# Attention stage of a hybrid backbone: where TensorE issues the first map of scores within a turn

## What is computed

```python
# differential attention: two maps of scores a head, 4 heads, 64 wide each
s = einsum('bqhmd,bkhmd->bhmqk', q, k) * DIFF_SCALE
p = softmax(s)
attn = p[:, :, 0] - lam * p[:, :, 1]
o = rms_norm(einsum('bhqk,bkhe->bqhe', attn, v)) * silu(gd)
# hyena, order 2, twice for each of 4 blocks of 128 channels
y = irfft(rfft(u, 2L) * rfft(filter)) + bias * u
```

## Time and profile before

| | |
|---|---|
| median of 3 runs | 3881.94 us (3874.04 to 3882.35) |
| profiled execution, its own time | 3885.88 us |
| its span, first to last instruction | 3884.1 us |
| mean granted TensorE clock | 0.949 |
| matmuls; DVE; ACT; GpSimd instructions | 18212; 4480; 1981; 782 |

### The profile page before, as it was taken

How to read it: one execution, slowest core, us unless ns; L and a number is a source line. 1 busy time by engine, 2 the same in 40 slices (tenths; PEclk the granted TensorE clock), 3 DMA queues, 4 the chain that set the end, 5 groups by cost and what they waited for, 6 DMA issues and landing times. The chain is left out here.

```text
span 3884.1 us, 48584 instructions
## 1 busy us (share of the span) xinstructions
PE 3384.3 (87%) x18212; PEld 2751.6 (71%) x18212; DVE 2470.1 (64%) x4480; ACT 1093.9 (28%) x1981; POOL 1067.4 (27%) x782
## 2 busy tenths in 40 slices
PE   6999999999868886886997899999999688858798
PEld 2787888888757775554783577888887587745477
DVE  4134577755369996885664324657775599968765
ACT  2111222212245454332210211222211455523321
POOL 4233334333212321210222423433433022232121
PEclk8999999999989998998998899999999799979899
DMA  5254223223173312344435155323322633133442
GB/s 208 65 155 147 80 91 96 86 89 97 53 204 98 84 58 71 118 113 132 146 97 206 58 122 174 99 78 103 95 90 62 199 90 93 43 107 110 128 143 69
DMA packets 414893, 423.34 MB, mean 109 GB/s; under 512 B 57040, under 2 KB 351440, under 8 KB 413506
## 3 DMA queue, kind: packets, MB, share of 16 engines
q1 hardware_dynamic: 368676, 315.22, 28.2%
q10 hardware_dynamic: 45984, 105.01, 7.7%
HBM read 287.76 MB, written 124.01 MB: 106 GB/s over the span
## 5 line engine op out<-in xcount | busy, mean ns | idle before, releaser
L754 PE MATMUL l_p_acc<-l_u_hi,l_w_hi 128*128 128x512 f32 (+1 forms) x2208 | 605.7, 376 | 22.8 <-PEq L158 9.0
L754 PE MATMUL l_p_acc<-l_u_hi,l_w_lo 128*128 128x512 f32 (+1 forms) x2208 | 587.3, 367 | 0.0
L754 PE MATMUL l_p_acc<-l_u_lo,l_w_hi 128*128 128x512 f32 (+1 forms) x2208 | 586.7, 367 | 0.0
L754 PEld LDWEIGHTS l_p_acc<-l_u_hi,l_w_hi 128*128 128x128 f32 x2208 | 383.8, 189 | 99.2 <-issue 25.2
L667 POOL TENSOR_TENSOR l_w_hi<-l_wt,l_p_zero 128x1024 fp32r<-128x1024 f32 x100 | 200.5, 2005 | 899.7 <-PE l_p_acc L754 744.1
L754 PEld LDWEIGHTS l_p_acc<-l_u_lo,l_w_hi 128*128 128x128 f32 x2208 | 380.8, 189 | 71.7
L754 PEld LDWEIGHTS l_p_acc<-l_u_hi,l_w_lo 128*128 128x128 f32 x2208 | 380.5, 189 | 71.6
L1506 PE MATMUL l_at_pS<-l_at_k_hi,l_at_q 128*128 128x512 f32 (+1 forms) x400 | 166.6, 416 | 133.1 <-ACT l_at_prob L1622 75.6
L669 POOL TENSOR_TENSOR l_w_lo<-l_wt,l_w_hi 128x1024 fp32r<-128x1024 f32 x100 | 265.3, 2653 | 7.8
L1740 DVE TENSOR_REDUCE l_at_nmax<-l_at_pS 128x1 f32<-128x1280 f32 (+1 forms) x144 | 197.4, 1371 | 103.0 <-PE l_at_pS L1507 99.0
L2457 PE MATMUL l_o_pA<-l_o_w_hi,l_o_o_hi 128*128 128x512 f32 x576 | 223.7, 407 | 42.7 <-DVE l_o_o_lo L2567 31.6
(11 more groups left out here) (331 smaller groups left out, 7058.5 us busy)
## 6 DMA issues: line engine op xcount, KB each, us to landing
l_wt<-w_in SPq DMA_DIRECT2D x104, 512.0 KB, 3.9
l_n_wa<-w_ada SPq DMA_DIRECT2D x10, 2048.0 KB, 16.5
kf_d<-l_p_R SPq DMA_DIRECT2D x72, 256.0 KB, 3.6
xbc_d<-l_p_fin ACTq DMA_DIRECT2D x28, 640.0 KB, 2.9
l_at_K<-kf_d SPq DMA_DIRECT2D x64, 256.0 KB, 2.9
l_o_rows<-w_out SPq DMA_DIRECT2D x32, 512.0 KB, 4.9
l_o_oT<-o_d SPq DMA_DIRECT2D x16, 1024.0 KB, 7.0
qk_d<-l_p_late ACTq DMA_DIRECT2D x12, 1280.0 KB, 4.6
```

What stands on the lines that cost most here:

```text
L754: mm = pe.matmul(acc[:, a:a + w], (w_hi, w_lo)[wp][m % 2][:, k], (u_hi, u_lo)[up][:, k, t0 + c:t0 + c + w], start=(k == n == 0), stop=(k = ...
```

## The change

At the end of turn `i`, between `turn_rows` and `backward(n)`, PE issues the first map of scores of unit `i + 1`; the call at the head of a turn is left for unit 0 alone. The number of instructions is the same, and so is the order on every other engine.

```diff
                 for i in range(NI):
                     n = step_of(i)
                     turning = batches[i - 2] if 2 <= i < NU + 2 else 0
+                    if i == 0:
+                        scores(i, 0)
                     if turning > 1:
                         turn(i - 2, 0, False)
-                    if i < NU:
-                        scores(i, 0)
                     if n is not None:
                         forward(n)
                     if turning > 2:
@@
                             pe.wait_ge(gated, i - 3)
                         turn_rows(r)
+                    if i + 1 < NU:
+                        scores(i + 1, 0)
                     if n is not None:
                         backward(n)
```

## The result

| | before | after |
|---|---|---|
| median, 4 runs each | 3882.14 us | 3913.99 us (3910.16 to 3920.37) |
| ratio after to before, 95% interval | | 1.0079 (1.0063 to 1.0095) |
| profiled execution, its own time | 3885.88 us | 3910.16 us |
| its span | 3884.1 us | 3908.4 us |

The account below looks back on a forecast made before the run. PE's closed ring from `exp` to `exp` was taken to bound ordinary turns, DVE's chain every fourth. Layer 1 13.4, layer 0 16.4 and clock 6.6 sum to 36.4 us over 3881.94: 3918.3 us, range 3898 to 3938.

Parts of the forecast that it names:

- The cover: Ordinary turns: only batch 0, no longer the map too, hides `copy_back` before the way there; 0.50 us a turn.
- The wait: Turn 21: the moved map's last piece waits 2.6 us for `exp(21, 1)`, ahead of the way back; 1.84 for turns 20 and 21.
- The turns with rows: There `turn_rows` already waits behind `maximum(i, 1)`, so the moved map finds its bank nearly free; two turns cost one 0.50.
- The clock: PE drops to 1.2 from 2.4 GHz behind two of three long waits; 4 x 1.65 = 6.6 us, bounds 0 and 9.9.
- heavy waits: Six waits of about 2.6 us where PE idled 1.09: turns 17, 21, 25, 29 in layer 1, 17 and 25 in layer 0.
- By layers: Covers and waits summed by groups of turns: layer 1 13.4 us, layer 0 16.4 us, together 29.8.
- Turns 34 to 38: Layer 0: the moved map delays batch 0, which starts ACT's chain to `exp`; 3.9 us, between 0 and 6.2.
- every turn falls: Rival: ordinary turns' idle of 1.57 also lowers the clock, some 30 more turns paying 1.65; 3968 us, chance 0.05.
- the 1.07 would swallow the gap: Rival: the 0.50 comes out of PE's idle at the last piece, leaving only the waits; 3889 us, chance 0.08.
- the maximum, coming sooner, would free `exp`: Rival: scores 2.15 us sooner let `exp(i, 0)` start sooner; 0.3 us in each of 60 turns, 3864 us, chance 0.05.
- PE's ring: Ordinary turn, `exp` to `exp`: 10.66 us, PE in all but 1.07 and 1.13; added PE idle lengthens the turn by as much.

Follow-up runs that it names:

- e1: Changed kernel, but the map back at its old place behind turns with n % 4 == 2 from turn 17 on; 3896.2 us, ratio 1.0028 to before.
- e3: Kernel before, with the next unit's first map moved behind the way back, still ahead of batch 0; 3886.0 us, ratio 1.0000.
- e4: Kernel before, with two of the first map's three pieces moved ahead of the way back, the last behind batch 0; 3889.0 us, ratio 1.0003.
- e2: Kernel before, with the map moved ahead of the way back only behind turns with n % 4 == 2 from turn 17 on; 3903.7 us, ratio 1.0046.
- e6: Changed kernel, with transposes and three value blocks filling PE's idle ahead of the second map's last piece; 3922.0 us, ratio 1.0099 to before.
- e5: Kernel before, with transposes and three value blocks filling PE's idle ahead of the second map's last piece; 3885.2 us, ratio 1.0007.
- e8: Kernel before; in turns with n % 4 == 2 from 9 on, two pieces of the next first map precede rows and way back; 3875.7 us, ratio 0.9977.
- e7: Kernel e5 plus the edit of e8; 3878.6 us, ratio 0.9978 to before.

## Why the prediction was right, point by point

**The cover.** Forecast 0.50 a turn, with the way there 0.86 behind batch 0. Measured 0.52 (10.66 to 11.18), 0.85, and in brackets the 0.25 of the earlier trace rows. That row, from the only turns of before in which this order already occurred, carried the largest term. `e1` shows that it costs alone, `e3` that it vanishes with the map behind the way back, `e4` that 0.59 of cover in place of 0.36 leaves 0.29 in an ordinary turn. Where DVE places the next `exp`, a smaller loss than this is absorbed (`e4`), and this one in part (`e1`: three lost covers cost 1.0 in four turns).

**The wait.** Forecast 2.6 us of idle and 1.84 for turns 20 and 21; measured 2.30 and 24.94 - 23.07 = 1.87. The idle was too large in the main because I held `exp(21, 1)` at its place against turn 20's start, 17.66; it came at 3301.61 - 3284.14 = 17.47. Already `exp(20, 1)` came 3.53 behind `exp(20, 0)` and not 3.71, released by DVE both times; that DVE had caught up in turn 20 is my reading of it. That 1.84 and 1.87 agree so closely is in part luck: from `exp(21, 1)` to the next turn's `exp` I had 7.25 and it took 7.47, as the last piece and the way there, each behind a wait, took 0.35 and 1.89 where I had 0.23 and 1.78. The two errors cancel. The turn behind took 11.26, 0.14 less than before and not 0.24, with 0.34 ahead of the way there in place of 0.25.

**The turns with rows.** Forecast: one 0.50 for two turns, an idle that shrinks to 1.6, and up to 3.3 us back. In turns 9 and 13 of layer 1 the idle was 1.59 and the turns went from 15.04 and 15.03 to 13.40 and 13.41: the whole 3.3 came back. The sum had left it out. That the shorter idle did it is likely and not shown turn by turn: with 2.10 the clock also held in turn 9 of `e2` and turn 13 of `e3`, where nothing had been changed ahead of that wait.

**The clock.** Forecast: the clock falls behind four of six heavy waits, at 1.65 each. It fell behind three. Windows behind the waits of turns 17, 21, 25, 29 of layer 1 (column PEclk is the one behind the five busy times):

```profile
3254.10:3258.10 4.00, 4.00 (x21) 4.00 (x22) 3.94 (x13) 0.06 (x1) 0.00 (x0) 0.57 0.01 4
...
3303.08:3307.08 4.00, 3.75 (x31) 3.51 (x32) 3.93 (x13) 1.63 (x6) 0.00 (x0) 1.00 0.04 12
...
3350.48:3354.48 4.00, 3.75 (x31) 3.51 (x32) 3.93 (x13) 1.65 (x6) 0.00 (x0) 1.00 0.00 0
...
3397.87:3401.87 4.00, 4.00 (x22) 3.90 (x22) 3.93 (x13) 0.26 (x1) 0.00 (x0) 0.62 0.00 0
```

The same idle of 2.30 gave 0.57 and 0.62 in two turns and 1.00 in two; of layer 0's two one fell. A turn whose clock fell took 15.37 and 15.18, else 13.76: 1.61 and 1.42. The Trainium skill (TensorE: Matmul & The Clock Gate, "HAM oscillation — how this bites in real kernels") describes a loop with a wait for a DMA of some 3 to 5 us in every round, where the clock falls in every round. The waits of 2.30 us here are shorter and did so in half of the rounds; those of 2.99 to 3.43 in `e2` did so in all six, those of 3.43 and 3.44 in `e6` in five of six.

**By layers.** Layer 1: forecast 13.4 without the clock, measured 14.3 with two falls (3.0) and the 3.3 back. Layer 0: forecast 16.4, measured 13.8 with one fall. Two errors of opposite sign lie in it. Turns 22 and 23, which I had counted at 0.5 each, became 3.8 shorter; they were long before, with idle and a low clock, and I had not asked why. Turn 13 cost 1.5, where I had 0, and turn 33, which I had left out of the six, 2.9. Turns 34 to 38 cost 2.9 where I took 3.9; of it 0.91 each are turns 34 and 38. The step that was mis-sized most, though the total stayed inside the range, is this one: the turns around short tiles were estimated, not read turn by turn.

**The rivals.** That every turn falls was wrong: ordinary turns, with 1.07 and 0.25 idle, had a clock of 1.00, as in turn 20. That the 1.07 would swallow the gap was wrong: both stand in the same turn. That the maximum, coming sooner, would free `exp`: ACT's copy of batch 1 still waited for PE (0.69) and `exp` still followed it at once. In `e5`, where PE was given that time, the sum of turns fell by 1.6 us only; PE and DVE are near to each other in these stages. My sentence that PE's ring sets an ordinary turn holds for adding to it, not for taking away, and over a group of four turns DVE's chain sets the sum: 45.14 us for turns 18 to 21 before, 45.10 in `e3`, 45.20 in `e4`, 45.12 in `e8`.

## What to carry to other kernels

Work on the bounding engine that stands between a producer and the consumer of its copy is a cover; before moving it, look for a place in the same trace where that order occurs already, and take the gap from the starts there. An instruction that waits for a late event belongs behind those in its queue that don't; cut it where its wait begins, and leave only the waiting piece behind. And count the turns one by one where another engine's chain absorbs or hands on a delay: in `e4` the price of the light turns disappeared in the heavy one, in `e1` what the heavy turn had absorbed came back in the next.

## What the runs showed of the hardware

The granted clock fell or held behind idle times of the same length. By idle time of PE ahead of the waiting instruction in heavy turns, over the executions profiled (turns 13 and 33 of layer 0 left out):

| idle, us | clock fell | where |
|---|---|---|
| 1.6 | 0 of 6 | turn 9 of layer 0, turns 9 and 13 of layer 1, in the changed kernel and `e1` |
| 1.82 to 1.87 | 0 of 4 | the same turns in `e4`, turn 9 of layer 0 in `e8` |
| 2.1 | 4 of 9 | turns 9 and 13 as above in before, `e2` and `e3` |
| 2.3 | 3 of 6 | the changed kernel |
| 2.44 to 2.59 | 3 of 7 | `e5`, ahead of the way back |
| 2.65 to 3.35 | 2 of 3 | turns 9 and 13 as above, `e7` |
| 2.99 to 3.43 | 6 of 6 | `e2` |
| 3.05 to 3.08 | 1 of 3 | turns 9 and 13 as above, `e6` |
| 3.43 to 3.44 | 5 of 6 | `e6` |
| 3.57 to 3.58 | 2 of 3 | turns 9 and 13 as above, `e5` |

So the earlier trace rows, with two of three, was a small sample; the longer idle times fell more often, but from 2.1 to 3.6 us the same length could go either way. In the kernel before and the changed one a fall cost 1.4 to 1.7 us of a turn; in turn 9 of `e5`, where the clock stayed low for longer, 2.9 (16.79 against 13.93 in turn 13). Of the largest gain of this study, `e8`, 3.3 of 12.1 us in the turns are those of two turns of layer 1 that kept the clock behind shorter idle times, with the wait for the other engine in turn 21 as long as before.
